# Far x tiles, x1 stores and a bias row moved in the queues of a hybrid decoder step

## What is computed

```python
h = rmsnorm(x, g_mix); proj = h @ w_in
s = einsum('gij,bnjgc->bnigc', w, vc) + b_s        # b_s: the bias row
merged = gate_a * (pa @ w_pool_out) + gate_b * (sg @ w_gmlp_out)
x = x + merged @ w_out                             # x1
h2 = rmsnorm(x, g_ffn)
x = x + (silu(h2 @ w_gate) * (h2 @ w_up)) @ w_down
y = rmsnorm(x, g_final)
```

## Time and profile before

| | |
|---|---|
| median of 3 runs | 758.9 us (758.84 to 761.04) |
| the profiled execution | 758.97 us |
| its span on the slowest core (core 3) | 756.8 us |
| spans of the eight cores | 745.9 to 756.8 us |
| PE busy | 731.1 us (97%) |
| DVE busy | 582.9 us (77%) |
| ACT busy | 377.2 us (50%) |
| POOL busy | 109.1 us (14%) |
| chain that ended last, PE's share | 82% |

### The profile page before, as it was taken

How to read it: one execution, slowest core, us unless ns; L and a number is a source line. 1 busy time by engine, 2 the same in 40 slices (tenths; PEclk the granted TensorE clock), 3 DMA queues, 4 the chain that set the end, 5 groups by cost and what they waited for, 6 DMA issues and landing times.

```text
span 756.8 us, 15077 instructions; the slowest of 8 cores (745.9 to 756.8 us)
## 1 busy us (share of the span) xinstructions
PE 731.1 (97%) x4771; PEld 431.0 (57%) x4771; DVE 582.9 (77%) x1304; ACT 377.2 (50%) x825; POOL 109.1 (14%) x185
## 2 busy tenths in 40 slices
PE   7999999999999999999979999999999999999995
PEld 3655455666666645456646665455666666654452
DVE  4789999998988885767557667975567776768986
ACT  3586756676766655775525552001555555522232
POOL 5244321000001011110111001000111100002121
PEclk9999999999999999999989999999999999999999
DMA  8997903140313369792994205771356442005762
GB/s 204 242 250 131 142 27 58 15 57 15 57 15 57 115 131 301 190 152 66 173 163 71 42 2 84 221 268 40 59 82 96 73 71 42 2 1 174 227 217 111
DMA packets 50973, 84.05 MB, mean 111 GB/s; under 512 B 24528, under 2 KB 24656, under 8 KB 50880
## 3 DMA queue, kind: packets, MB, share of 16 engines
q0 software_dynamic: 15984, 29.11, 25.9%
q1 hardware_dynamic: 34478, 53.39, 24.6%
q10 hardware_dynamic: 434, 0.60, 0.3%
HBM read 87.90 MB, written 19.49 MB: 142 GB/s over the span
## 4 chain that ended last, share of the span: by engine, by line
PE 82%; DMA 8%; DVE 5%; issue 2%; ACT 1%; SPq 1%; POOL 1%; DVEq 0%; ACTq 0%; POOLq 0%
PE ps L558 80%; DMA Sx<-wpk 3%; DMA Rg<-wpk 3%; DMA hT<-Sx 2%; SPq L625 1%; DVE hT L592 1%; DVE Fr L592 1%; DVE X L600 1%; PE ps L1169 1%; DVE Pr L592 1%; ACT Fr L581 1%; DVE Sx L592 1%; PE ps L742 0%; DVE X L592 0%; POOL Sx L625 0%
## 5 line engine op out<-in xcount | busy, mean ns | idle before, releaser
L581 ACT ACTIVATE Fr<-ps 128x344 f32<-128x344 f32 (+2 forms) x456 | 203.9, 464 | 161.3 <-PE ps L558 131.7
L558 PE MATMUL ps<-hT,Rg 128*128 128x344 f16 x1440 | 247.2, 310 | 0.5
L592 DVE TENSOR_TENSOR Fr<-Fr,ps 128x344 f32<-128x344 f32 (+2 forms) x356 | 175.6, 509 | 68.3 <-ACT Fr L581 42.3
L558 PE MATMUL ps<-Sx,Rg 128*128 128x344 f16 x1080 | 192.4, 310 | 5.6 <-DVE Rg L592 3.9
L558 PEld LDWEIGHTS ps<-hT,Rg 128*128 128x128 f16 x1440 | 140.4, 98 | 73.4 <-issue 3.4
L558 PEld LDWEIGHTS ps<-Sx,Rg 128*128 128x128 f16 x1080 | 104.6, 98 | 60.6 <-issue 9.6
L592 DVE TENSOR_TENSOR X<-X,ps 128x512 f32<-128x512 f32 (+1 forms) x131 | 85.5, 670 | 21.4 <-PE ps L558 19.0
L625 POOL DMA_DIRECT2D Rg<-wpk x60 | 31.8, 531 | 354.4 <-PE ps L558 352.8
L581 ACT ACTIVATE junk<-X 128x1025 f16<-128x1025 f32 (+3 forms) x43 | 44.1, 1024 | 77.0 <-DVE X L592 59.8
L558 PE MATMUL ps<-Mr,Pr 128*128 128x512 f16 x352 | 81.0, 379 | 0.0
L581 ACT ACTIVATE Fr<-Fr 128x344 f16<-128x344 f32 x108 | 52.6, 490 | 55.4 <-DVE Fr L592 55.2
(11 more groups left out here) (133 smaller groups left out, 685.5 us busy)
## 6 DMA issues: line engine op xcount, KB each, us to landing
Rg<-wpk POOLq DMA_DIRECT2D x60, 256.0 KB, 4.0
X<-xp SPq DMA_DIRECT2D x22, 512.0 KB, 15.5
X<-xd SPq DMA_DIRECT2D x18, 512.0 KB, 5.1
Mr<-wpk POOLq DMA_DIRECT2D x33, 256.0 KB, 6.3
yp<-X SPq DMA_DIRECT2D x14, 512.0 KB, 2.9
xd<-Pr SPq DMA_DIRECT2D x12, 512.0 KB, 5.1
Pr<-xp SPq DMA_DIRECT2D x10, 512.0 KB, 11.5
xd<-X SPq DMA_DIRECT2D x8, 512.0 KB, 5.6
```

Of the source, the lines that this page charges most:

```text
L558: ins = e.matmul(out=ap, lhsT=l, rhs=rr, start=(start and i == 0), stop=(stop and i == len(pairs) - 1), skip_group_check=more)
L581: return e.activation(out=P.r(out), in_=P.r(in_), func=func, scale=scale, **kw)
L592: return P.add(eng, lambda e: e.tensor_tensor(out=P.r(out), in0=P.r(a), in1=P.r(b), op=op), reads=[a, b], writes=[out], dur=vdur(n, per), ...
```

## The change

Three edits. The loads of positions 9 to 16 wait for the norm's last step (the transpose; for the sample tile at position 6 the copy behind PE's transpose) of the position seven places before, instead of the load of tile 10. The stores of positions 12 to 16 join those of 10 and 11 behind the last transpose, and no longer wait for FFN weights. The planner is told that the bias row lands 3.5 us later than it assumed.

```diff
-        dma('act', bs_row[0:1, :], cst[0:1, C_BS:C_BS + 512], 'c4', rows(1, 2048), -9.8)
+        dma('act', bs_row[0:1, :], cst[0:1, C_BS:C_BS + 512], 'c4', rows(1, 2048), -9.8).slack = 3500.0
...
+        tn = []
         for n_, t in enumerate(wo_order):
             pr = 2000.0 + 10.0 * n_
             if t < NT:
-                xload(t, 1950.0 + n_, [x_dma[10]] if n_ > 6 else [wo7])
+                xload(t, 1950.0 + n_, [tn[n_ - 7]] if n_ > 8 else [x_dma[10]] if n_ > 6 else [wo7])
...
             tlast = norm(t, gffn, pr + 1.0, t < NT)
+            tn.append(tlast)
             if t < NT and 6 < n_ < 10:
                 xstore(t, pr + 100.0, tlast)
         for n_, t in enumerate(wo_order):
-            if 10 <= n_ < 12:
+            if 10 <= n_:
                 xstore(t, 2200.0 + n_, tlast)
...
-                        if gi == 0 and f == 3:
-                            for i_ in range(12, 17):
-                                xstore(wo_order[i_], 2990.0 + i_, Bf[f]['ld'])
```

## The result

The changed kernel takes **748.8 us** (median of five runs, 748.6 to 749.4) where the kernel before took 758.9; the ratio is 0.986, 95% interval 0.984 to 0.988. Forecast were 750.0 us and a range of 747 to 755.

A forecast was written before the change was run, and what follows sets the result against it. PE, busy 97% of the span, was taken as the bound, with local waits and a lower clock as the loss: 758.97 - 1.78 - 8.34 + 0.3 + 0.6 + 0.2 = 749.95, forecast 750.0 us, range 747 to 755.

The forecast's parts named there:

- The floors: PE's time without losses: 59.9 us from output projection to FFN, 165.9 us from there to the first down projection's sample matmuls.
- x loads: Output projection: with two loads ahead instead of ten, transposes land near 3.2 us and PE's 1.78 us wait goes.
- The +0.3 for the sample tile's own chain: Output projection: the sample tile, reached by DVE one add later, becomes next late and costs 0.3 us.
- the 7 that I named as the sign: Output projection: if the forecast is right, no transpose takes over some 7 us to land.
- x1 stores: Start of the FFN: seven stores end by 355.7, before the first weight reload at 356.8, and 8.34 us go.
- the thin margin of 1.1 us: Start of the FFN: time by which the stores clear the first weight reload at 250 GB/s.
- The rival that stores run into the weights: FFN: at half rate the stores run 13.6 us into the reload; half the 8.34 us returns, 754.2 us; chance 0.14.
- POOL and DVE: FFN weight loads: PE has 8 us to spare at f=4 and f=5; DVE may stand for f=4's sums, costing 0.6 us.
- Bias row: Head of the kernel: two f32 matmuls (2.04 us) and a 0.69 us cast move later, taken as +0.2 us.
- No change, by POOL's queue: FFN: POOL's own queue, not the stores, delays f=4's load; only the first stretch gains, 757.7 us; chance 0.07.
- Slower, by held loads: Output projection: load, add, norm, transpose form a loop; loads come 11.3 us late, 764.6 us; chance 0.07.
- the threshold of 17.3 us: Held-load loop: transpose and load together must take over 17.3 us (22.7 - 5.4) before loads come late.

The follow-up runs named there:

- the stores alone: Only the x1 stores moved behind the last transpose, old loads and bias row, against the kernel before: 753.8 and 754.5 us, ratio 0.994.
- the block of three: The changed kernel with three far x loads in a block in place of two: 748.2 to 749.7 us, ratio 0.987 to the kernel before.
- the loads or the bias row alone: Only the x loads held, or only the bias row's planned landing moved, against the kernel before: 750.7 to 752.3 us (0.991), or 757.9 to 760.7 us (1.002).
- the lag of five: The changed kernel with held loads waiting for the tile five places before, not seven: 754.7 to 756.5 us, ratio 0.995 to the kernel before.

## Why the prediction was right

- **The floors.** 59.9 and 165.9 us were read as PE's own time, from cores 3 and 6. The first is met to 0.02 us on all cores. The second came out at 166.35: a new gap of 0.21, and 166.14 busy on core 6 where before 165.86 were; the planner's order of PE's products has moved. The tail, which I had taken as untouched, is 0.5 us shorter, so in the total the two cancel by luck: they are no trade, since the stores alone and the block of three have the shorter tail (251.0 to 251.4 us) and a second stretch of 166.06 on their best cores. The tail is short in those two and the change and not with the loads or the bias row alone or with the lag of five (251.5 to 251.9), so it goes with some order of the planner; which one stays open.
- **x loads.** Right, term and mechanism: the 1.78 us went, by ACT's wait for a late transpose. The +0.3 for the sample tile's own chain was not there (the bracket is empty). My figure of 3.2 us for the transposes was low, 5.0 at the median and 8.1 at most on core 3, above the 7 that I named as the sign.
- **x1 stores.** Right. They were gone by 354 in place of 355.7, as 381 GB/s were reached where I took 250 (which was no rate, see the end), so the thin margin of 1.1 us was 2. The 8.34 us went, low clock included. The rival that stores run into the weights fell with it.
- **POOL and DVE.** The 0.6 us for f=4's sums was not there: DVE did not wait, and PE's gap of 0.21 is one behind ACT, at the start of the FFN. That the second stretch still came out within 0.11 us is luck, since 0.21 and 0.28 from elsewhere stood in its place. The way there was mis-read too: I had the first five weight loads landed by 369, one after the other at 2.4 us; POOL issues them as PE frees the buffers, the last at 366.10, and they landed in 3.8 to 6.4 us each, the second half of f=4 by 371.3. The cover was thinner than told, and it held.
- **Bias row.** Neither confirmed nor refuted: +0.14 in the mean first mark, 0.41 on core 3, -0.50 to +0.87 over the cores, which is scatter as far as these runs tell.
- **No change, by POOL's queue.** Refuted as the cause by the stores alone; its order may explain a part, as above.
- **Slower, by held loads.** Refuted at seven places, and seen at three to five, with the planner's other orders not separated: nearer than the chance of 0.07 told. The longest transpose and load that I added, 14.5 and 14.1, were the block's own; but the sum behind the threshold of 17.3 us left out SP's own order, and by that sum five places were about enough, which cost 6 to 8 us.

The sum, 749.95, was 1.31 us above the profiled execution: 0.36 in the first stretch (mostly the +0.3), 0.11 in the second, and 1.05 in what no term held, the tail and the time outside the span, less 0.21 by which core 3 started later than forecast.

The block of three is the nearest thing to a better version: second stretch 166.06 to 166.13, no gap on any core. Its ratio, 0.987 (0.985 to 0.989), cannot be told from that of the change. No run beat it.

## What to carry to other kernels

When one core of several loses time in a stretch where another does not, the difference prices the loss and the better core gives the floor; here that gave the result to 0.2%, in part by errors that cancelled. A bulk transfer that is not needed yet is not free: hold it back until the short transfers on the critical path are through, and count its bytes, not its queue. Then check the hold as a loop, with every instruction on the issuing queue that stands ahead of the held load.

## What the runs showed that I had not expected

- A second queue does not protect a short transfer: with ten loads by POOL and transposes alone on SP the longest transpose was issued 3 us earlier and landed no earlier, 17.0 to 19.0 us after its issue, against 14.5 to 16.3 when all shared SP's queue.
- The last microseconds are steep. From three to six loads in a block the longest transpose rises by some 2 us, and the time by 4 to 6 (with six loads it is one execution).
- Stores of 0.5 MB ran at 312 and 381 GB/s beside nothing else; the 250 of the window before were no rate at all: two stores, 1.05 MB, make 262 GB/s over 4 us however fast they are.
